# Attention by pairs of heads, set between the projection units that it does not yet need: two transformer blocks on one Trainium2 core

## The reference

```python
# block one, layer l; h, hc: normed and modulated x and context
u = h @ w_in[l]                       # 1024 -> 2560: conv, pool, q, k, v
y = concat([gated_conv_mixer(u[:256], u[256:512], u[512:768]),
            multiscale_pool_mixer(u[768:1024]),
            neighbourhood_attention(q, k, v, kc, vc, rpb[l])]) @ w_out[l]
# the context stream (layer 0 only): the same with context_attention,
# softmax(q k^T / 8) v over its 256 keys, 8 heads of 64

# block two, layer l
proj = h @ w_in_2[l]                  # 30 tiles of 128 for q, k, v; 24 for gates
o_a = swa_sink_attention(rope(q), rope(k), v, sinks)     # 8 query, 2 kv heads
o_b = stick_breaking_attention(q, k, v)                  # 8 heads
o_c = moba_attention(rope(q), rope(k), v)                # 8 heads
g = sigmoid(gates + b_gate)
x = x + (g0 * (o_a @ wb[0]) + g1 * (o_b @ wb[1]) + g2 * (o_c @ wb[2])) @ w_out
```

## Time and profile before

| | before |
|---|---|
| time, median of 3 runs | 2989.01 us (2987.98 to 2989.61) |
| the profiled execution | 2993.86 us, its span 2992.0 us |
| mean granted clock of TensorE | 0.961 |
| busy: PE, PEld | 93%, 79% |
| busy: DVE, ACT, POOL | 51%, 37%, 14% |
| attention, block one, layers 0 and 1 | 99.1 and 70.6 us |
| attention with gates, block two, layers 0 and 1 | 158.7 and 156.0 us |

### The profile page before, as it was taken

The page is one execution under the profiler, slowest core; times in us unless marked ns, Lnnn a source line. Parts: engine busy times, 40 slices in busy tenths (PEclk is TensorE's granted clock), DMA queues, the critical chain, the costliest instruction groups (busy, mean ns, idle before and its releaser), DMA issues.

```text
span 2992.0 us, 44068 instructions
## 1 busy us (share of the span) xinstructions
PE 2770.4 (93%) x16482; PEld 2350.1 (79%) x16482; DVE 1533.6 (51%) x2330; ACT 1103.6 (37%) x1676; POOL 426.3 (14%) x411
## 2 busy tenths in 40 slices
PE   4999999888999999999988999898889999988998
PEld 2777777746777776778876699798689999868998
DVE  3333335474333334333354655566567775666776
ACT  2212223143222223222241444435446553444554
POOL 4101012114101012000031110201012020101201
PEclk8999999989999999999999899899899999999999
DMA  7555343204535445353233156464245656324563
GB/s 245 176 169 169 120 154 88 84 1 107 171 118 175 133 123 165 122 169 118 81 110 91 48 158 183 134 176 120 64 127 153 184 163 182 113 71 132 155 185 113
DMA packets 653883, 400.28 MB, mean 134 GB/s; under 512 B 11898, under 2 KB 614954, under 8 KB 653610
## 3 DMA queue, kind: packets, MB, share of 16 engines
q1 hardware_dynamic: 651914, 395.01, 43.5%
q0 software_dynamic: 1824, 3.29, 0.7%
HBM read 397.21 MB, written 1.05 MB: 133 GB/s over the span
## 4 chain that ended last, share of the span: by engine, by line
PE 85%; DVE 7%; ACT 3%; issue 2%; POOL 1%; DMA 1%; SPq 0%; ACTq 0%; DVEq 0%; POOLq 0%
PE bank L1620 20%; PE bank L1621 20%; PE bank L1622 20%; PE bank L1591 3%; PE bank L1592 3%; PE bank L1593 3%; PE bank L1521 2%; PE bank L1734 2%; PE bank L1680 2%; PE bank L1770 1%; PE bank L1682 1%; PE bank L1681 1%; DVE T L1149 1%; DVE H_hi L1153 1%; PE bank L1780 1%
## 5 line engine op out<-in xcount | busy, mean ns | idle before, releaser
L981 DVE TENSOR_TENSOR w_lo<-raw,w_hi 128x1024 fp32r<-128x1024 f32 x609 | 785.4, 1290 | 641.3 <-ACT w_hi L707 640.4
L1620 PE MATMUL bank<-H_hi,w_hi 128*128 128x256 f32 (+1 forms) x2800 | 927.1, 331 | 16.8 <-POOL H_lo L1425 11.2
L1621 PE MATMUL bank<-H_hi,w_lo 128*128 128x256 f32 (+1 forms) x2800 | 920.0, 329 | 0.0
L1622 PE MATMUL bank<-H_lo,w_hi 128*128 128x256 f32 (+1 forms) x2800 | 919.4, 328 | 0.0
L707 ACT ACTIVATE w_hi<-raw 128x1024 fp32r<-128x1024 f32 x609 | 639.4, 1053 | 666.8 <-PE bank L1622 540.2
L1620 PEld LDWEIGHTS bank<-H_hi,w_hi 128*128 128x128 f32 x2800 | 534.8, 191 | 88.8 <-issue 30.5
L1622 PEld LDWEIGHTS bank<-H_lo,w_hi 128*128 128x128 f32 x2800 | 535.2, 191 | 47.2
L1621 PEld LDWEIGHTS bank<-H_hi,w_lo 128*128 128x128 f32 x2800 | 535.1, 191 | 43.8
L1415 POOL TENSOR_TENSOR G_lo<-g,G_hi 128x512 f32 (+3 forms) x132 | 141.5, 1072 | 1432.3 <-ACT G_hi L763 1123.3
L1620 PE MATMUL bank<-G_hi,w_hi 128*128 128x512 f32 (+1 forms) x792 | 266.6, 337 | 0.0
L1621 PE MATMUL bank<-G_hi,w_lo 128*128 128x512 f32 (+1 forms) x792 | 266.2, 336 | 0.0
(11 more groups left out here) (180 smaller groups left out, 3584.0 us busy)
## 6 DMA issues: line engine op xcount, KB each, us to landing
raw<-ffn_w_in SPq DMA_DIRECT2D x176, 512.0 KB, 3.8
raw<-w_in SPq DMA_DIRECT2D x148, 512.0 KB, 3.7
quad_ring<-w_mod SPq DMA_DIRECT2D x66, 1024.0 KB, 6.7
raw<-w_up SPq DMA_DIRECT2D x88, 512.0 KB, 3.9
...
```

Source lines behind the costliest of these rows:

```text
L981: dve.tensor_tensor(w_lo[:, slot, :], raw[:, slot, :], w_hi[:, slot, :].bitcast(F32), ALU.subtract).then_inc(lo_done, 1)
L1620: pe.matmul(o, wh, xh[:, k, 0:width], start=k == 0, stop=False)
L1621: pe.matmul(o, wl, xh[:, k, 0:width], start=False, stop=False)
L1622: ins = pe.matmul(o, wh, xl[:, k, 0:width], start=False, stop=k == kk - 1)
```

## The change

**Which units are stored ahead.** Block one stores 8 tiles ahead of the attention (q and k in layer 0, k and v in layer 1); block two stores 6 (swa's). All others become a phase of kind "fill", 12 units in block one and 48 in block two, whose weights are fetched and split like any other's, but which is walked inside the attention. Fill units use banks 0 and 1; VectorE empties those that are stored, ScalarE the gates.

**Attention by pairs of heads.** Scores of a pair lie in banks 4 and 5, transposed weights in 6 and 7, outputs in bank 3, and bank 2 (MISC) serves v's transposes and the rotation. VectorE's and ScalarE's operations cover both heads where they can: one add, one maximum, one copy of the transposed weights. There is one set of score banks instead of four. In block one q is scaled when it is stored, so the scores need no scaling.

**An order by ticks.** `block1_items` and `block2_items` write a list of items by tick, with one unit (a half one in block one's layer 0) per tick, sorted within a tick by `IN_TICK`; every engine walks the same list. A job's weights, turn and values come 1, 3 and 4 half units after its scores in layer 0, and 1, 2 and 3 units after them elsewhere. The convolution is cut in two items, the pooled product comes after the last exponential, and the three sigmoids stand at ticks 41, 43 and 48 of block two.

**The output projection's start.** Mixer and attention outputs of block one go to `U_r` (a float32r view of `U`) instead of `H_hi` and `H_lo`, which the fill units still read. Its first three units are done together, k by k in the order `Y_ORDER`, around the last turn and values.

**GpSimd** loads the next layer's bias table after the last maximum instead of after the last output, rotates two tiles per operation, and starts pooling when tile 7 is stored.

The core of the diff:

```diff
+SWA_TILES = 6
+Y_HI = (0, 1, 16, 17, 8, 9, 10, 11)
+Y_LO = (2, 3, 18, 19, 12, 13, 14, 15)
+Y_ORDER = (4, 5, 6, 0, 1, 2, 3, 7)
+Y_JOINT = 3
...
-            gemm("store", 12, KD, S, plain_source(w_in[layer]), moving="h", dst="U", f0=0)
             gemm("store", 8, KD, 512, plain_source(w_in[layer], 1536), moving="h", dst="U", f0=12)
         else:
-            gemm("store", N_IN, KD, 512, plain_source(w_in[layer]), moving="h", dst="U", f0=0)
-        plan.append(("mixers", dict(layer=layer, streams=1 if last else 2)))
-        plan.append(("attend", dict(block=1, layer=layer, streams=1 if last else 2)))
+            gemm("store", 8, KD, 512, plain_source(w_in[layer], 1024), moving="h", dst="U", f0=8, scale_first=True)
...
-             norm_next=n_norm[0])
+        tiles = ((8, 9, 10, 11) if last else (16, 17, 18, 19)) + (6, 7, 0, 1, 4, 5, 2, 3)
+        fill = gemm("fill", 12, KD, width, tile_source(w_in[layer], tiles), moving="h", dst="U", tiles=tiles)
+        mixed = dict(layer=layer, streams=1 if last else 2, fill=fill)
+        plan.append(("mixers", mixed))
+        attend = dict(block=1, layer=layer, streams=1 if last else 2, fill=fill, mixed=mixed)
+        plan.append(("attend", attend))
+        attend["after"] = gemm("residual", KD, KD, width, plain_source(w_out[layer]), seg=layer * 3 + 1, stats=True,
+                               moving="y", norm_next=n_norm[0], attend=attend)
...
-        gemm("store", N_QKV, KD, S, plain_source(w_in_2[layer]), moving="h", dst="U2", f0=0)
-        gates_phase = gemm("gate", N_GATE, KD, S, plain_source(w_in_2[layer], N_QKV * P), moving="h", layer=layer)
-        plan.append(("attend", dict(block=2, layer=layer, streams=1, gates=gates_phase)))
+        gemm("store", SWA_TILES, KD, S, plain_source(w_in_2[layer]), moving="h", dst="U2", f0=0)
+        fill = gemm("fill", N_QKV - SWA_TILES + N_GATE, KD, S, plain_source(w_in_2[layer], SWA_TILES * P), moving="h", dst="U2",
+                    tiles=tuple(range(SWA_TILES, N_QKV + N_GATE)), layer=layer)
+        plan.append(("attend", dict(block=2, layer=layer, streams=1, fill=fill)))
...
+    IN_TICK = ("values", "sb_values", "weights", "turn", "scores", "sb_scores", "sb_log", "sb_remain", "out", "sb_out",
+               "rope_add", "swap", "rope", "turn_v", "bias", "conv_in", "conv_out", "sigmoid", "unit")
...
+    def block1_items(at_):
+        two, layer = at_["streams"] == 2, at_["layer"]
+        ticks = {}
+
+        def at(tick, what, arg):
+            ticks.setdefault(tick, []).append((what, arg))
+        parts = 2 if two else 1
+        for q in range(at_["fill"].n):
+            for part in range(parts):
+                at(q * parts + part, "unit", (q, part, parts))
+        for j in range(6):
+            at(j // 3, "bias", j)
+        for j in range(4):
+            at(3 + 2 * j if two else j, "turn_v", j)
+        jobs = []
+        for pair in range(4):
+            if two:
+                jobs.append(new_job("ctx", pair, 0, layer))
+            jobs += [new_job("near", pair, qt, layer) for qt in range(2)]
+        for m, j in enumerate(jobs):
+            if two:
+                add_job(at, j, 2 * m, 1, 3, 4)
+            else:
+                add_job(at, j, 2 + 5 * m // 4, 1, 2, 3)
+        end = at_["fill"].n * parts
+        at(end - 3 if two else end - 1, "conv_in", None)
+        at(end, "conv_out", None)
+        items = ordered(ticks)
+        last_turn = max(i for i, item in enumerate(items) if item[0] == "turn")
+        last_value = max(i for i, item in enumerate(items) if item[0] == "values")
+        tail = items[last_turn + 1:last_value]
+        steps = [("mix_step", k) for k in Y_ORDER]
+        items = items[:last_turn] + steps[0:1] + [items[last_turn]] + steps[1:2] + [("pooled", None)] + tail + \
+            items[last_value:] + steps[2:]
+        at_["jobs"] = jobs
+        return items
...
+        for q in range(at_["fill"].n):
+            at(q, "unit", (q, 0, 1))
+        for tick, tiles in ((0, (4,)), (1, (0, 1)), (2, (2, 3)), (16, (18, 19)), (18, (22, 23)), (20, (20, 21)), (22, (24, 25))):
+            r = dict(tiles=tiles, r=counts["rope"])
+            counts["rope"] += 1
+            at(tick, "rope", r)
+            at(tick + 1, "rope_add", r)
+        at(1, "swap", None)
+        for tick, j in ((1, 0), (11, 1), (13, 2), (23, 3), (25, 4)):
+            at(tick, "turn_v", j)
+        jobs = [new_job("swa", pair, 0, layer) for pair in range(4)]
+        for m, j in enumerate(jobs):
+            add_job(at, j, 3 + 2 * m, 1, 2, 3)
+        sb = []
+        for pair in range(4):
+            z = dict(pair=pair, n=counts["sb"], first=pair == 0)
...
+            at(12 + pair, "sb_scores", z)
+            at(16, "sb_log", z)
+            at(18 + pair, "sb_remain", z)
+            at(20 + pair, "sb_values", z)
+            at(20 + pair, "sb_out", z)
...
+        for m, j in enumerate(moba):
+            j["first"] = m == 0
+            add_job(at, j, 24 + 4 * m, 1, 2, 3)
+        for i, tick in enumerate((41, 43, 48)):
+            at(tick, "sigmoid", i)
...
-        def gate_evict(ph, q):
-
...
+            ph = at_["fill"]
+            if part == 0:
+                split_ahead(ph, q % 4, q // 4)
+            if part == parts - 1:
+                f = ph.more["tiles"][q]
+                src = bank[q % 2][:, 0:ph.width]
+                if at_["block"] == 2 and f >= N_QKV:
+                    act.wait_ge(acc_done, ph.start + q + 1)
+                    act.activation(gates[:, f - N_QKV, :], src, ACT.Identity,
+                                   bias=vec("b_gate", at_["layer"] * N_GATE + f - N_QKV)).then_inc(acc_free, 1)
...
+            n, c0, what = j["n"], j["c0"], j["what"]
+            act.wait_ge(max_done, n + 1)
+            at_least(act, pt_done, n - 1)
+            if j["first"]:
+                act.wait_ge(pv_done, j["free_z"])
+            if what == "near":
...
+                    c = c0 + (2 * e + si if what == "ctx" else 2 * si + e)
+                    ins = act.activation(probs[:, n % 2, e, a:b], score2[:, e, a:b], ACT.Exp, bias=neg_max[:, c:c + 1],
+                                         accum_out=row_sum[:, c:c + 1])
...
+        def act_turn(j):
+
+            n = j["n"]
+            w = 512 if j["what"] in ("near", "ctx") else 384
+            act.wait_ge(pt_done, n + 1)
+            at_least(act, pv_done, j["free_t"])
+            act.activation(probs_t[:, n % 2, :, 0:w], turn2[:, :, 0:w], ACT.Copy).then_inc(pt_copy, 1)
+
+        def act_sb_scores(z):
+            j, n = z["pair"], z["n"]
+            act.wait_ge(sb_scaled, n + 1)
+            act.activation(sb_e[j][:, :, :], sb_z[:, j, :, :], ACT.Abs).then_inc(sb_log, 1)
+            act.wait_ge(sb_log, z["log0"] + 2 * j + 1)
+            act.activation(sb_e[j][:, :, :], sb_e[j][:, :, :], ACT.Exp, scale=-1.0).then_inc(sb_log, 1)
...
+                    dve.wait_ge(bias_done, at_["bias0"] + 6)
+                dve.tensor_tensor(score2[:, :, 0:S], score2[:, :, 0:S],
+                                  bias_t[:, 2 * pair:2 * pair + 2, rr:rr + 4, :].rearrange("p h r k -> p h (r k)"),
+                                  ALU.add).then_inc(mask_done, 1)
+                dve.wait_ge(mask_done, j["masked"])
+                dve.tensor_reduce(neg_max[:, c0:c0 + 2], score2, AX.X, ALU.max, negate=True).then_inc(max_done, 1)
...
+        def dve_weights(j):
+
+            n, c0, what = j["n"], j["c0"], j["what"]
+            ns = 2 if what == "near" else 4
+            dve.wait_ge(exp_done, n + 1)
+            if what == "swa":
+                dve.tensor_tensor(row_sum[:, c0:c0 + 4], row_sum[:, c0:c0 + 4], sink_e[:, c0:c0 + 4], ALU.add) \
+                   .then_inc(inv_step, 1)
+                dve.wait_ge(inv_step, j["inv"] - 1)
+            dve.reciprocal(row_inv[:, c0:c0 + ns], row_sum[:, c0:c0 + ns]).then_inc(inv_step, 1)
+            dve.wait_ge(inv_step, j["inv"])
...
+            for a, b, si in cols:
+                for e in range(2):
+                    c = c0 + (2 * e + si if what == "ctx" else 2 * si + e)
+                    ins = dve.tensor_scalar(probs[:, n % 2, e, a:b], probs[:, n % 2, e, a:b], row_inv[:, c:c + 1], None, ALU.mult)
+            ins.then_inc(p_ready, 1)
...
+        def dve_split_out(j, hi, lo):
+            src = out_cols(j)
+            dve.wait_ge(pv_done, j["pv"])
+            dve.tensor_copy(hi, src).then_inc(o_step, 1)
+            dve.wait_ge(o_step, j["out"])
+            dve.tensor_tensor(lo, src, hi.bitcast(F32), ALU.subtract).then_inc(o_done, 1)
...
+        def dve_unit(at_, q, part, parts):
+
+            ph = at_["fill"]
+            if part == 0:
+                split_ahead(ph, q % 4, q // 4)
+            if part == parts - 1:
...
+                if at_["block"] == 1:
+                    dve.wait_ge(acc_done, ph.start + q + 1)
+                    if 8 <= f < 12:
+                        dve.tensor_scalar(U[:, f, 0:ph.width], src, SCALE, None, ALU.mult).then_inc(acc_free, 1)
```

(42 more changed lines are left out.)

1048 lines of the change are left out of this document (515 added, 533 removed).

## The result

The changed kernel takes 2889.86 us (median of 4 runs, 2884.06 to 2891.24), the kernel before 2988.93 beside it: a ratio of 0.9665, 95% interval 0.9648 to 0.9682. That is 99 us less; 91 were forecast (2898). The two profiled executions are 104.5 us apart in span (2992.0 and 2887.5), since before's profiled execution lies 4.9 above its median; stage by stage the comparison is with that number.

A forecast was written before the change was run, and what follows sets the result against it. TensorE (PE), busy 93% of the span, was taken as the bound, with some 84 us idle in the attention stages. Gains of 42, 25, 14 and 11 sum to 92 us, giving 2898 us; range 2856 to 2945.

The forecast's parts named there:

- First stage: Block one, two streams, 99.1 us: PE binds at 8.7 us per job; 48.4 of work, 8.7 of waits; gain 42.
- Second stage: Block one, one stream, 70.6 us: the loop binds; PE work 34.5, waits and low clock 16.2, 5 hidden; gain 25.
- The loop: Second stage: maximum, exp, w_hi, w_lo, eviction, weights, next maximum take 7.6 us a tick against PE's 6.2; waits 6.
- Third and fourth stage: Block two, 158.7 and 156.0 us: gate units 70.8, attention items 42.3, other units 1.7, waits 30; gains 14 and 11.
- The waits of block two: Each block-two stage: swa 10, stick-breaking 9, moba 7, rotation and k's swap 2, start and end 1 us.
- swa: Block two: a job's chain over two ticks takes 11.2 us against PE's 8.5; four jobs wait 10.
- the low clock: Block two: stretches of PE at low clock add 1.3 us, making 30 with the waits.
- 170 changes: Switches between half-wide and full matmuls: no extra taken; at a further 0.1 us each, 17 us less gain, 2915.
- PE binds everywhere: Rival: loops of stages 2 to 4 are slack, giving back some 55 of 76 us of waits; 2843; chance 0.08.
- VectorE becomes the bound: Rival: VectorE and ScalarE work in order with one score buffer; waits twice as large, 85 more; 2983; chance 0.08.
- Pairs don't run side by side: Rival: among units, a pair's scores and values double, 83 us, some 37 hidden in waits; 2944; chance 0.04.
- Slower by the clock: Rival: short waits lower the clock of projections in the mixed stretches, a third at half clock; 3038; chance 0.04.

The follow-up runs named there:

- e10: e1 with v's first turn in tick 4, VectorE's logs behind their tick's eviction, and the output projection's first steps behind the last values; 2820.91 us.
- e1: The changed kernel with ScalarE making a unit's w_hi ahead of the tick's exponentials, Abs, Exp or Ln instead of behind them; 2837.26 us.
- e9: e10 with ScalarE emptying every fill unit, the stored ones too; 2813.18 us.
- e11: The changed kernel with a second maximum over the same 1024 elements ahead of the first in each near job of block one; 2904.9 us.

## Why the prediction was right

**First stage, 42 forecast, 45.1 measured.** PE binds as said: 8.65 us from one near job's scores to the next (605.25 and 613.90), 8.7 forecast.

```profile
605.25 1.13 PE L1912 MATMUL psum<-U 64*128 64x256 f32 x8
...
613.90 1.13 PE L1912 MATMUL psum<-U 64*128 64x512 f32 x4
```

The wait at the tail came in two pieces: 2.2 ahead of values and 0.9 at the first output step, 3.1 where 4 stood; behind it PE ran at the lower level (transposes of 1.91 us instead of 1.03), which the sum had not priced.

**Second stage, 25 and 24.1.** The loop was named with its members in order and sized at 7.6 us a tick; it is 6.87. The tail was 6.6, it is 6.5. That the loop's waits come to 7.1, near the 6 forecast, is in part luck: an excess of 0.7 a tick instead of 1.4 would give 4 over six intervals, less the free tick. Two things that the sum lacked make up for it. The values wait for VectorE's split of an earlier output (in bank 3), which stands behind w_lo, the eviction and the weights:

```profile
1583.01 0.42 DVE L1399 TENSOR_TENSOR U_r<-psum,U_r 128x256 fp32r<-128x256 f32 x1
...
1583.54 1.09 PE L1955 MATMUL psum<-probs_t,vt 128*64 128x128 f32 x16 [2.83 <-issue]
```

And one interval between maxima is 7.94 (1587.50 to 1595.44): the weights take 1.92 us in it, beside GpSimd's pooling, instead of 0.88.

**Third and fourth stage, 14 and 11 forecast, 19.8 and 17.2 measured: the step that failed.** Two terms were mis-sized, in opposite directions. The waits of block two were sized at 28.7 us and are 18.5. By items: swa 10, measured 5.8; stick-breaking and its logs 9, measured 4.2; moba 7, measured 4.6; rotation 2, measured 3.2. The members of the swa loop are right and in the right order, but a job's turn follows the last one after 10.1 us and not after 11.2:

```profile
1927.64 0.88 PE L1930 MATMUL psum<-const,probs 128*128 128x128 f32 x6 [0.77 <-DVE probs L1391]
...
1937.74 0.87 PE L1930 MATMUL psum<-const,probs 128*128 128x128 f32 x6 [1.45 <-DVE probs L1391]
```

From start to start, the chain's w_lo take 1.14 us each instead of 1.29, the evictions 0.33 instead of 0.43 (both twice), the sinks 0.19 instead of the 0.5 that I had guessed, the exponentials 1.70 instead of 1.9: that is the missing microsecond. Less than half of it is an error of method: I had added up the durations of records, and on VectorE the next instruction starts before a record ends (in the tick above w_lo lasts 1.23 and its successor starts 1.14 later, the eviction 0.42 and 0.33). The rest are guesses, and a mean of w_lo (1.29) over places where GpSimd slows it. An error of 1 us a job decides here, since only the excess over PE's 8.5 counts: it nearly halves the waits. For stick-breaking PE ran ahead over four ticks, as the prediction allowed, and paid 1.8 at the end.

The other term is the low clock, priced at 1.3. In the third stage's mixed stretch PE is busy 189.6 us, where the sum has 185.6 (48 units of 2.95, 42.3 and 1.7). That is not more work: in e10 the same stretch runs at clock 1.00 throughout, and PE is busy 182.65.

```profile
1867.54:2052.37 184.83, 182.65 (x1473) 168.47 (x1473) 128.92 (x206) 100.76 (x171) 8.53 (x7) 1.00 0.47 137
```

So the items were counted 3 us too high, and some 7 us (189.6 less 182.65) are what the lower level cost: in the changed kernel the clock is 0.90 from 1892 to 1910, 0.85 from 1910 to 1920 and 0.94 from 1960 to 1990, behind waits of 2.6, 2.1 and 1.8. Ten us of waits too many and almost six of low clock too few cancel in part, and that is luck. The fourth stage is alike (waits of 18.6, clock 0.98).

What a unit costs depends on its neighbours. Between two items on the full array it took 2.95. Scores and values use half the array (64 of its rows or columns): after a transpose and ahead of values a unit takes 3.03, between two such items 3.06:

```profile
1948.90 0.36 PE L1849 MATMUL psum<-H_hi,w_hi 128*128 128x256 f32 x1
...
1951.73 0.28 PE L1851 MATMUL psum<-H_lo,w_hi 128*128 128x256 f32 x1
1951.93 0.87 PE L1955 MATMUL psum<-probs_t,vt 128*64 128x256 f32 x8
...
1953.59 0.39 PE L1849 MATMUL psum<-H_hi,w_hi 128*128 128x256 f32 x1
```

(the next scores start at 1956.65). A unit's matmuls start 0.12 apart, the values 0.20 after its last: going over to half the array costs 0.08, coming back 0.03. The Trainium skill, "TensorEngine Tiling (Array Packing)", Key Properties, says that TensorE drains when the mode changes; the trace agrees, and one way it costs nearly the 0.1 us at which the prediction had tried it. The prediction said that the rows leave no such rest; they do, a unit ahead of stick-breaking's values took 3.05 (2092.94 to 2095.99 in the earlier trace rows). Over its 170 changes it is some 9 us (an estimate, 85 times 0.11), in part paid before too. It doesn't show in the total, as the other items were priced too high.

**Busy time.** It falls by 72 us and not 50. The 50 didn't follow from the prediction's own terms: PE's 76.1, 58.0, 134.0 and 132.4 us against 48.4, 34.5, 114.8 and 114.8 are 88 less. Over the four stages it falls by 74.6 (26.3, 22.1, 13.5, 12.8). How much of that is less work, and how much is attention work that no longer runs at 1.2 GHz (clocks of 0.83 and 0.86 in the earlier trace rows), no run separates.

**The rivals.** *PE binds everywhere* was priced at 2843, by giving back 55 us of waits. It is not what the change does. e1 comes to 2837 by a change of order alone, but still waits 19.4 us in the mixed stretches, so that the numbers are so near is chance; e9 is the kernel that is nearest to the rival's state. *VectorE becomes the bound* by its load is refuted by e1 (the same work for VectorE, 53 us less) and half right by e11 (its queue has no slack in the second stage): the bound is its order of work with ScalarE's, not its load, 52% of the span. *Pairs don't run side by side*: the scores of a pair take 1.06 us (605.25 and the unit's start at 606.31). *Slower by the clock*: 0.94 to 0.97 in all stages.
